# Where the input buffer and the weight tensors begin: a shift of 224 bytes in a two-block transformer kernel

## The chip, the cores and the metric

The kernel runs on one core of one Trainium2 chip. The metric is the device time of one execution in microseconds (us). A core has a matrix engine (TensorE, in the profile PE, and PEld for its loading of weights), VectorE (DVE), ScalarE (ACT), GpSimd (POOL) and a sync engine (SP) that issues most transfers. On-chip memory has 128 partitions; a tensor takes the same range of bytes in each, and its place in this text is the byte at which that range begins.

## The reference

Two transformer blocks on a sequence of 512 tokens of 1024 features, all in float32. Cut to what matters:

```python
def first_block(x, ...):
    h = rms_norm(x, norm_mix_pre)
    proj = h @ w_in                       # retention and sparse attention inputs
    mix = concatenate([retention(...), nsa(...)]) @ w_out
    x = x + rms_norm(mix, norm_mix_post)
    h = rms_norm(x, norm_ffn_pre)
    return x + rms_norm(conv_ffn(h, ffn_w_up, ffn_conv, ffn_w_down), norm_ffn_post)

def second_block(x, ...):
    for layer in range(2):                # 0: mLSTM and spatial gating, 1: latent attention
        x = x + mixer(rms_norm(x, ...))
        h = rms_norm(x, ...)
        x = x + square(relu(h @ ffn_w1)) @ ffn_w2
    return rms_norm(x, final_norm)
```

Most of the work is the dense products with the weight matrices.

## The kernel before

The features lie on the partitions and the 512 tokens along them, so an activation is eight tiles of 128 x 512. The weights are laid out beforehand as 296 panels of 128 x 1024 float32. They pass through a fixed line of four stations:

1. SyncE issues the transfer of a panel (512 KB, 4096 bytes for each partition) into slot `panel % 4` of `raw` (line 504), once VectorE is done with the panel that was there. The first four are issued by hand (lines 489 to 498), the first of them in two halves of 512 columns, between the eight tiles of the input `x_in`.
2. ScalarE copies the panel into a rounded high part, `w_hi` (`split`, line 1564), once TensorE has read the panel that held that half.
3. VectorE writes what the rounding lost, `w_lo = raw - w_hi` (`low`, line 2225).
4. TensorE multiplies. Each product of two float32 tiles is three matmuls, high x high, high x low and low x high (`product`, lines 695 to 697); a panel is eight such triples, 24 matmuls.

In nearly all products a 128 x 128 piece of the weights is the stationary operand, which is loaded ahead of the matmul, and an activation (`h_hi`, `h_lo`, `hid_hi`, `hid_lo`, ...) of 512 columns is the moving one. In those that yield values by tokens (`token_major`, line 723) it is the other way round. Tile names in the profile are "result<-operands"; of the two operands of a matmul the first is the moving one.

`w_hi` and `w_lo` have two halves each. Two more such buffers are free in parts of the kernel: `w_third` for the compression weights and for some panels ahead, `w_fourth` for panels ahead of the feed-forward and the gate. The compression matmuls (lines 1151 and 1152) take gathered activations `xg` as the stationary operand, of 126 and 62 columns, and `w_third` as the moving one.

Tensors are placed one behind another in the order in which `sb` makes them (lines 187 to 290). The places that matter here, modulo 256 bytes:

| tensor | begins past a multiple of 256 by, before | after |
|---|---|---|
| `small` | 128 | 128 |
| `masks`, `raw`, `w_hi`, `w_lo` | 224 | 0 |
| `ev`, `h_hi`, `h_lo`, `tmp`, `sq`, `x`, `hid_hi`, `hid_lo`, `q_hi`, `cq_hi` | 224 | 224 |
| `w_third`, `w_fourth` | 128 | 128 |
| `xg` | 0 | 0 |

Every piece of a weight tensor that a matmul reads begins a multiple of 512 bytes behind the tensor's start, so it has the same place modulo 256. `w_third` and `w_fourth` differ from `w_hi` because 8 spare columns (`front_spare`, `ahead_spare`) stand before them.

`small` holds the constants and gains by columns; its last 8, `g_mix_pre`, come in a transfer of their own before the rest, on ScalarE's queue (lines 1686 and 1687). The columns called `spare` in it are read by nothing. `masks` feeds small matmuls that add masks in the attention stages.

Of the kernel before, what the change touches and what calls it, by code (L numbers as in the profile page):

```python
# [13 lines left out]
F32 = mybir.dt.float32  # L14
# [7 lines left out]
P = 128  # L22
# [40 lines left out]
def columns(*parts):  # L63
    at, out = 0, {}
    for name, n in parts:
        out[name] = (at, n)
        at += n
    return out, at
# [3 lines left out]
    ("ident", 128), ("ones", 128), ("g_mix_post", 8), ("g_ffn_pre", 8), ("g_ffn_post", 8),  # L72
    ("gn", 4), ("cmp_pos", 64), ("conv0", 132), ("g_ab", 8), ("conv1", 40), ("gate_b", 1), ("g_head", 4),
    ("g_c", 8), ("g_cq", 3), ("g_ckv", 2), ("g_ffn1", 8), ("g_ffn2", 8), ("g_final", 8), ("freq", 1),
    ("rope_sign", 1), ("minus_half", 16), ("head_row", 4), ("shift_rows", 3), ("g_v", 4), ("spare", 57), ("g_mix_pre", 8))
FIRST, FIRST_N = columns(("rope_c", 512), ("rope_s", 512), ("cmp_c", 32), ("cmp_s", 32), ("decay", 2048))
SECOND, SECOND_N = columns(("sgu_b", 512), ("ws_t", 512))
MASKS, MASKS_N = columns(("ident", 128), ("k_q", 128), ("q_k", 128), ("cmp_q_k", 128), ("cmp_k_q", 512))
# [95 lines left out]
def build(nc, A):  # L174
    with ExitStack() as ctx:
        build_in(nc, A, ctx)


def build_in(nc, A, ctx):
    def sb(name, shape, dt, c=ctx):  # L180
        return c.enter_context(nc.sbuf_tensor(name, shape, dt))
# [7 lines left out]
    raw = sb("raw", [P, 4, PANEL], F32)  # L189
    w_hi = sb("w_hi", [P, 2, PANEL], F32R)  # L190
    w_lo = sb("w_lo", [P, 2, PANEL], F32R)
    ev = sb("ev", [P, 4, S], F32)
    h_hi = sb("h_hi", [P, KD, S], F32R)
    h_lo = sb("h_lo", [P, KD, S], F32R)
# [5 lines left out]
    spare = sb("spare", [P, 32], F32)  # L200
# [3396 lines left out]
```

## Time and profile before

| | |
|---|---|
| three runs, median (lowest to highest) | 1883.29 us (1883.24 to 1883.4) |
| the profiled execution: span from first to last instruction | 1881.6 us |
| what the median of the runs has over that span | 1.7 us |
| TensorE busy, share of the span | 98% |
| its loading of weights | 79% |
| VectorE, ScalarE, GpSimd | 61%, 40%, 12% |
| moved by the transfers | 165.68 MB, mean 88 GB/s |

The span is the profile's own time of one execution; the runs are timed from outside and include what lies around it. Busy TensorE doesn't mean TensorE at its peak, as matmuls are pipelined: how fast it works is read from the distance between the starts of neighbouring matmuls. The loading of weights (PEld) goes beside the matmuls.

### The profile page before, as it was taken

Reading aid. Unit: us, or ns where it says so; the run is one execution under the profiler, and the core shown is the slowest. Engines: PE = TensorE matmul, PEld = TensorE weight load, DVE = VectorE, ACT = ScalarE, POOL = GpSimd, SP = SyncE. Lnnn points to the kernel's source line nnn. Section 1 sums busy time; section 2 is a strip of 40 time slices with the busy share of each in tenths; the row PEclk is TensorE's granted clock in tenths of the full one; section 3 lists DMA queues with packets and bytes.
Section 4 is the critical chain, followed back from the end, with each engine's and each line's share of the span. In section 5 each row is a group of like instructions: output and inputs, shape, how many; then the busy total and the mean of one; then the engine's idle time right before and its main releaser. Section 6 shows DMA issues by size and latency. Waiting matters only on the chain.

```text
span 1881.6 us, 24672 instructions
## 1 busy us (share of the span) xinstructions
PE 1841.5 (98%) x8818; PEld 1481.6 (79%) x8818; DVE 1155.1 (61%) x1651; ACT 743.9 (40%) x1099; POOL 226.6 (12%) x228
## 2 busy tenths in 40 slices
PE   8999999999999999999999999999999999999998
PEld 6787558888888887887888888887666788888887
DVE  7867876784765778777543434476777553444344
ACT  6365334442432454655432232334544342323232
POOL 0021453000000030000000000003477200000000
PEclk9999999999999999999999999999999999999999
DMA  6332022233333233311333333332110123333332
GB/s 215 92 133 68 1 79 90 84 94 102 92 99 101 90 113 90 90 57 56 96 101 98 93 101 94 95 100 79 46 34 25 55 90 101 95 95 100 92 98 90
DMA packets 48217, 165.68 MB, mean 88 GB/s; under 512 B 5376, under 2 KB 7424, under 8 KB 48000
## 3 DMA queue, kind: packets, MB, share of 16 engines
q1 hardware_dynamic: 46512, 161.27, 28.3%
q10 hardware_dynamic: 1616, 3.22, 0.5%
q8 instruction: 56, 0.92, 0.2%
q14 instruction: 33, 0.27, 0.0%
HBM read 162.38 MB, written 2.10 MB: 87 GB/s over the span
## 4 chain that ended last, share of the span: by engine, by line
PE 85%; DVE 9%; ACT 3%; issue 2%; POOL 1%; DMA 0%; DVEq 0%; ACTq 0%; SPq 0%; POOLq 0%
PE ps L695 25%; PE ps L697 25%; PE ps L696 25%; PE ps L1089 2%; DVE w_lo L2225 1%; PE ps L989 1%; DVE qk_c L2995 1%; POOL x L608 1%; ACT w_hi L1564 1%; DVE tmp L2262 1%; PE ps L917 1%; PE ps L970 1%; PE ps L1059 1%; PE ps L1355 0%; PE ps L886 0%
## 5 line engine op out<-in xcount | busy, mean ns | idle before, releaser
L1564 ACT ACTIVATE w_hi<-raw 128x1024 fp32r<-128x1024 f32 x279 | 296.1, 1061 | 760.7 <-PE ps L697 760.4
L695 PE MATMUL ps<-h_hi,w_hi 128*128 128x512 f32 (+1 forms) x1288 | 507.9, 394 | 8.1 <-DVE w_lo L2506 7.6
L697 PE MATMUL ps<-h_hi,w_lo 128*128 128x512 f32 (+1 forms) x1288 | 499.0, 387 | 0.0
L696 PE MATMUL ps<-h_lo,w_hi 128*128 128x512 f32 (+1 forms) x1288 | 498.9, 387 | 0.0
L2225 DVE TENSOR_TENSOR w_lo<-raw,w_hi 128x1024 fp32r<-128x1024 f32 x279 | 345.5, 1238 | 119.7 <-ACT w_hi L1564 118.3
L695 PEld LDWEIGHTS ps<-h_hi,w_hi 128*128 128x128 f32 x1288 | 242.5, 188 | 62.1 <-DVE w_lo L2506 7.6
L697 PEld LDWEIGHTS ps<-h_hi,w_lo 128*128 128x128 f32 x1288 | 242.3, 188 | 50.0
L696 PEld LDWEIGHTS ps<-h_lo,w_hi 128*128 128x128 f32 x1288 | 242.6, 188 | 49.2 <-issue 1.9
L695 PE MATMUL ps<-hid_hi,w_hi 128*128 128x512 f32 (+1 forms) x716 | 273.6, 382 | 1.7 <-DVE w_lo L2225 0.9
L697 PE MATMUL ps<-hid_hi,w_lo 128*128 128x512 f32 (+1 forms) x716 | 272.6, 381 | 0.0
L696 PE MATMUL ps<-hid_lo,w_hi 128*128 128x512 f32 (+1 forms) x716 | 272.6, 381 | 0.0
L2440 DVE TENSOR_TENSOR x<-x,ps 128x512 f32<-128x512 f32 (+2 forms) x82 | 55.3, 675 | 187.9 <-PE ps L697 187.8
L695 PEld LDWEIGHTS ps<-hid_hi,w_hi 128*128 128x128 f32 x716 | 134.6, 188 | 29.0 <-DVE w_lo L2225 2.0
L696 PEld LDWEIGHTS ps<-hid_lo,w_hi 128*128 128x128 f32 x716 | 134.6, 188 | 25.8
L697 PEld LDWEIGHTS ps<-hid_hi,w_lo 128*128 128x128 f32 x716 | 134.6, 188 | 25.7
L3189 DVE SCALAR_TENSOR_TENSOR ev<-ps,tmp 128x512 f32<-128x512 f32 x64 | 44.1, 692 | 156.6 <-PE ps L697 152.9
L535 POOL TENSOR_TENSOR r<-r,small 128x2 f32<-128x2 f32 x6 | 4.2, 704 | 730.9 <-DVE r L2329 730.9
L530 POOL TENSOR_TENSOR r<-r,small 128x4 f32<-128x4 f32 x8 | 8.1, 1014 | 508.0 <-DVE r L2275 508.0
L2880 DVE TENSOR_REDUCE mla_negm<-ps 128x1 f32<-128x512 f32 x64 | 41.2, 686 | 15.6 <-PE ps L1059 14.9
L1875 ACT ACTIVATE pr<-ps 128x512 f32<-128x512 f32 x48 | 27.7, 597 | 52.9 <-PE ps L975 40.9
L2928 DVE TENSOR_TENSOR ev<-ps,tmp 128x512 f32<-128x512 f32 x44 | 30.4, 692 | 28.1 <-PE ps L697 26.6
L695 PE MATMUL ps<-w_hi,h_hi 128*128 128x512 f32 (+1 forms) x128 | 47.1, 368 | 0.3 <-DVE w_lo L2225 0.2
(435 smaller groups left out, 2547.6 us busy)
## 6 DMA issues: line engine op xcount, KB each, us to landing
raw<-in_panels SPq DMA_DIRECT2D x295, 512.0 KB, 3.6
x_in<-in_x SPq DMA_DIRECT2D x8, 256.0 KB, 5.5
x<-in_x ACTq DMA_DIRECT2D x1, 2048.0 KB, 9.7
out<-y SPq DMA_DIRECT2D x16, 128.0 KB, 1.8
first<-in_first SPq DMA_DIRECT2D x1, 1568.0 KB, 11.4
raw<-in_panels SPq DMA_DIRECT2D x2, 256.0 KB, 4.6
second<-in_second ACTq DMA_DIRECT2D x1, 512.0 KB, 3.5
small<-in_small ACTq DMA_DIRECT2D x1, 328.0 KB, 4.2
```

Of the source, the lines that this page charges most:

```text
L608: nc.gpsimd.tensor_tensor(x[:, k, at], x[:, k, at], tmp[:, k % 2, at], ALU.add).then_inc(x_ready, 1)
L695: nc.tensor.matmul(out, a[0], b[0], start=start, stop=False)
L696: nc.tensor.matmul(out, a[0], b[1], start=False, stop=False)
L697: return nc.tensor.matmul(out, a[1], b[0], start=False, stop=stop)
L1089: last = nc.tensor.matmul(ps[64 * a:64 * a + 64, pair_bank(p), cols_of(half)], mla_v[:, kt, n, :], weights_tile(n, kt)[:, cols_of(half)], ...
L1564: nc.scalar.activation(w_high(panel, i), raw[:, panel % 4, :], ACT.Copy).then_inc(w_hi_ready, 1)
L1875: nc.scalar.activation(prob(m), ps[:, 4 + m % 2, :], ACT.Exp, scale=0.125).then_inc(block_exp, 1)
L2225: signal(V.tensor_tensor(w_low(panel, i), raw[:, panel % 4, :], w_high(panel, i).bitcast(F32), ALU.subtract), w_lo_ready, wait=False)
L2440: signal(V.tensor_tensor(x[:, k, at], x[:, k, at], bank, ALU.add), done)
L2880: signal(V.tensor_reduce(mla_negm[:, n % 2, t:t + 1], ps[:, 2 + t % 2, :], AX.X, ALU.max, negate=True), mx_done, wait=False)
L2928: signal(V.tensor_tensor(src, bank, inv_b, ALU.mult), tile_out)
L3189: signal(V.scalar_tensor_tensor(ev[:, k % 4, :], bank, 0.0, inv_b, ALU.max, ALU.mult), tile_out, wait=False)
```

## The change

The unread columns `spare` in `small` shrink from 57 to 1, and a tensor of 56 float32 columns that nothing uses is put behind `w_lo`. So `masks`, `raw`, `w_hi` and `w_lo` begin 224 bytes earlier, and all tensors from `ev` on stay where they were. `g_mix_pre` moves with the end of `small`. No instruction is added, removed or put elsewhere; the transfer of `small` has 56 columns less.

```diff
@@ -72,7 +72,7 @@
     ("ident", 128), ("ones", 128), ("g_mix_post", 8), ("g_ffn_pre", 8), ("g_ffn_post", 8),
     ("gn", 4), ("cmp_pos", 64), ("conv0", 132), ("g_ab", 8), ("conv1", 40), ("gate_b", 1), ("g_head", 4),
     ("g_c", 8), ("g_cq", 3), ("g_ckv", 2), ("g_ffn1", 8), ("g_ffn2", 8), ("g_final", 8), ("freq", 1),
-    ("rope_sign", 1), ("minus_half", 16), ("head_row", 4), ("shift_rows", 3), ("g_v", 4), ("spare", 57), ("g_mix_pre", 8))
+    ("rope_sign", 1), ("minus_half", 16), ("head_row", 4), ("shift_rows", 3), ("g_v", 4), ("spare", 1), ("g_mix_pre", 8))
@@ -189,6 +189,7 @@
     raw = sb("raw", [P, 4, PANEL], F32)
     w_hi = sb("w_hi", [P, 2, PANEL], F32R)
     w_lo = sb("w_lo", [P, 2, PANEL], F32R)
+    behind_weights = sb("behind_weights", [P, 56], F32)
     ev = sb("ev", [P, 4, S], F32)
     h_hi = sb("h_hi", [P, KD, S], F32R)
```

## Rows read from the trace of the kernel before

**Rows 1.** The page: its first lines, and the chain that ended last.
```profile
span 1881.6 us, 24672 instructions
PE 1841.5 (98%) x8818; PEld 1481.6 (79%) x8818; DVE 1155.1 (61%) x1651; ACT 743.9 (40%) x1099; POOL 226.6 (12%) x228
...
PE 85%; DVE 9%; ACT 3%; issue 2%; POOL 1%; DMA 0%; DVEq 0%; ACTq 0%; SPq 0%; POOLq 0%
PE ps L695 25%; PE ps L697 25%; PE ps L696 25%; PE ps L1089 2%; DVE w_lo L2225 1%; PE ps L989 1%; DVE qk_c L2995 1%; POOL x L608 1%; ACT w_hi L1564 1%; DVE tmp L2262 1%; PE ps L917 1%; PE ps L970 1%; PE ps L1059 1%; PE ps L1355 0%; PE ps L886 0%
```

**Rows 2.** Waits: waiter <- releaser, us in total, times, longest us; SPq is SyncE's queue.
```profile
ACT w_hi L1564 <- PE ps L697: 760.4, 234, 7.5
ACT h_hi L1613 <- DMA raw<-in_panels: 2.2, 1, 2.2
SPq L504 <- DVE w_lo L2225: 1591.5, 277, 94.7
```

**Rows 3.** Timeline, TensorE, 512 columns: start us, duration us, instruction; first, last of seven.
```profile
1699.94 0.39 PE L695 MATMUL ps<-h_hi,w_hi 128*128 128x512 f32 x1
...
1701.30 0.39 PE L695 MATMUL ps<-h_hi,w_hi 128*128 128x512 f32 x1
```

**Rows 4.** The same, 256 columns, weights in w_hi and w_lo; first and last of ten.
```profile
301.02 0.28 PE L696 MATMUL ps<-h_lo,w_hi 128*128 128x256 f32 x1
...
302.10 0.28 PE L696 MATMUL ps<-h_lo,w_hi 128*128 128x256 f32 x1
```

**Rows 5.** Instructions with w_hi: x count, duration ns min/median/max, first and last start.
```profile
L695 PEld LDWEIGHTS ps<-h_hi,w_hi x1288: 186/188/334, 7.6 to 1825.5; 128*128 128x128 f32 x184
...
L695 PE MATMUL ps<-hid_hi,w_hi x716: 278/389/499, 409.7 to 1871.1; 128*128 128x512 f32 x165, 128*128 128x256 f32 x14
...
L695 PE MATMUL ps<-w_hi,h_hi x128: 290/389/470, 33.7 to 788.5; 128*128 128x512 f32 x96, 128*128 128x288 f32 x32
...
L695 PE MATMUL ps<-aq_hi,w_hi x64: 389/389/501, 871.7 to 918.7; 128*128 128x512 f32 x64
```

**Rows 6.** Timeline, 256 columns, weights in w_third and w_fourth; first and last of 31.
```profile
694.79 0.28 PE L695 MATMUL ps<-h_hi,w_third 128*128 128x256 f32 x1
...
698.39 0.28 PE L695 MATMUL ps<-h_hi,w_third 128*128 128x256 f32 x1
```

**Rows 7.** Timeline, xg stationary, w_third moving: first of eight, and the matmul behind them.
```profile
135.70 0.28 PE L1151 MATMUL ps<-w_third,xg 128*126 128x256 f32 x1
...
136.63 0.39 PE L695 MATMUL ps<-h_hi,w_hi 128*128 128x512 f32 x1
```

**Rows 8.** Timeline, 512 columns, just after a stall; first and last of six.
```profile
704.24 0.40 PE L695 MATMUL ps<-h_hi,w_hi 128*128 128x512 f32 x1
...
705.40 0.39 PE L697 MATMUL ps<-h_hi,w_lo 128*128 128x512 f32 x1
```

**Rows 9.** Instructions that read raw: duration ns min/median/max.
```profile
L1564 ACT ACTIVATE w_hi<-raw x279: 1042/1063/1072, 9.5 to 1859.3; 128x1024 fp32r<-128x1024 f32 x140
L2225 DVE TENSOR_TENSOR w_lo<-raw,w_hi x279: 1210/1226/2183, 10.6 to 1860.5; 128x1024 fp32r<-128x1024 f32 x140
L1564 ACT ACTIVATE w_third<-raw x11: 1042/1064/1070, 63.9 to 677.4; 128x1024 fp32r<-128x1024 f32 x11
L2225 DVE TENSOR_TENSOR w_third<-raw,w_third x11: 1209/1224/1227, 65.4 to 678.5; 128x1024 fp32r<-128x1024 f32 x11
```

**Rows 10.** Transfers by line: x count, KB each, median us from issue to landing.
```profile
raw<-in_panels SPq DMA_DIRECT2D x295, 512.0 KB, 3.6
...
small<-in_small ACTq DMA_DIRECT2D x1, 328.0 KB, 4.2
```

**Rows 11.** The chain of the start: start us, us, what.
```profile
1.20 4.07 DMA raw<-in_panels
...
7.62 0.80 PE ps L695
```

**Rows 12.** Stretch: us, busy (x) of PE, PEld, DVE, ACT, POOL, clock, DMA share, GB/s.
```profile
0.00:8.00 8.00, 0.38 (x1) 0.38 (x2) 1.79 (x3) 3.81 (x6) 1.54 (x8) 1.00 0.79 269
```

## The prediction

> **What bounds the kernel now.** I read the profile from the outside in: shares of engines, waits by engine, then the single matmuls, because a change that moves operands and nothing else can only act through the duration of single instructions and transfers. TensorE is busy 98% of a span of 1881.6 us, and 85% of the chain that ended last is on it [rows 1]. Three quarters of that chain is one helper, lines 695 to 697. The engines that prepare the weights wait for it: ScalarE's copy into `w_hi` waits 760.4 us for TensorE's readings, 234 times, so some 3.2 us before each; the transfers of panels wait 1591.5 us for VectorE to free a slot of `raw`. For a transfer instructions wait only at the start, the longest 2.2 us, once [rows 2]. So the reader is to see a queue in which weights are always early, and one thing that counts: how long TensorE takes per matmul.
>
> In a quiet stretch six matmuls of 512 columns take 1701.30 - 1699.94 = 1.36 us, 226.7 ns each [rows 3]. With 256 columns nine take 302.10 - 301.02 = 1.08 us, 120.0 ns each [rows 4]. The difference, 106.7 ns for 256 columns, is one column per cycle at 2.4 GHz; 226.7 less twice that leaves 13.3 ns, and so does 120.0 less once that: a surcharge per matmul, whatever its length. This surcharge is what the change could touch: if it were the price of where an operand begins, it would be worth tens of microseconds.
>
> **The change, part by part.** `spare` inside `small` goes from 57 to 1 columns, 56 x 4 = 224 bytes, and `behind_weights` puts 224 bytes back behind `w_lo`. `masks`, `raw`, `w_hi` and `w_lo` move down by 224 bytes; before they began 224 bytes past a multiple of 256, now on one. `ev`, `h_hi`, `hid_hi` and the rest stay 224 past. No instruction, wait or queue changes.
>
> (a) **Weights as the stationary operand**, 1288 + 716 + 64 = 2068 triples, 6204 matmuls [rows 5] (and some smaller groups). The trace has tensors at another place already: `w_third` and `w_fourth` lie 128 past a multiple of 256. With them as weights and `h_hi`, `h_lo` moving, thirty matmuls of 256 columns take 698.39 - 694.79 = 3.60 us, 120.0 ns each [rows 6], the same as with `w_hi` [rows 4]. Moving the weights by 96 bytes against the moving operand cost and brought nothing. A place at 256 itself is shown by `xg` alone (it begins on a multiple of 256), stationary under `w_third`: eight matmuls of 256 columns take 136.63 - 135.70 = 0.93 us, 116 ns [rows 7]. Those load 126 and 62 columns, not 128, so I don't read the 4 ns as alignment; they are the lower bound: 4 x 6204 = 25 us at most. The upper bound is a cadence as after a stall, 5 matmuls in 705.40 - 704.24 = 1.16 us, 232 ns [rows 8]: 5.3 x 6204 = +33 us. I take 0, by rows 6, nearest in size, operands and engine. The load itself lasts 188 ns [rows 5] beside a matmul of 226.7 ns, so 39 ns of cover are left; a load shorter by any amount brings nothing.
>
> (b) **Weights as the moving operand**: 128 triples, 384 matmuls [rows 5] (and a few of the third block). Here the moving operand itself lands on 256. Bound: all 13.3 ns go, 384 x 13.3 = 5.1 us; or, as in (a), +5.3 ns, 2.0 us. I take 0: `w_third` is the moving operand of rows 7, and 9.3 ns of surcharge are still there.
>
> (c) **ScalarE and VectorE.** ScalarE's copy has a median of 1063 ns into `w_hi`, 1064 into `w_third`; VectorE's difference 1226 and 1224 [rows 9]. Both read `raw` and write elsewhere, and a shift of the one side by 96 bytes moves them by 2 ns or less. Cover: the 3.2 us before each copy. If it were gone, both hold about 1% of the chain each [rows 1]; even 2% of some 38 us is 0.8 us. I take 0.
>
> (d) **Transfers.** A panel lands 3.6 us after its issue [rows 10], with four slots and a panel of 24 x 226.7 ns = 5.4 us of matmuls; steady transfers are hidden, and a faster one starts the next no sooner, as the queue waits for VectorE. On the path is the first half panel alone, 4.07 us from issue to landing [rows 11], with everything after it up to the first matmul at 7.62 us. It shares the engines with the transfer of `small`, now 300 KB instead of 328 [rows 10]: 28 KB at the 269 GB/s of that stretch [rows 12] are 0.1 us. Bounds: nothing, if that transfer is not in its way, and 0.4 us, a tenth of the landing. I take -0.1.
>
> The trace cannot show how a transfer treats a destination off 256, as nothing large is written on one. The Trainium skill, "DMA: Bandwidth & Descriptors", section "How a descriptor splits into AXI transactions", says that a transfer off a 256-byte boundary pays for the bytes before its start. By it a row of 2048 bytes would go from 71 beats to 64 and the start would gain up to 0.4 us, an estimate from that page; the sum would be 1882.9 instead of 1883.2.
>
> (e) `masks` feed small matmuls of 128 columns and less in the attention stages, `small` keeps its start. 0.
>
> **Sum.** 1881.6 - 0.1 = 1881.5 us of span. The median of three runs, 1883.29, lies 1.7 us above the span; I keep that: 1883.2 us. What a measurement of this kernel can tell from no change is 0.2%, 3.8 us.
>
> **The rivals.**
> - *The surcharge is the stationary operand's place.* 13.3 ns x 6204 = 83 us would go, 1883.3 - 83 = 1800; with the 4 ns of rows 7, 1858. For: a surcharge that doesn't grow with the length looks like a start cost. Against: rows 4 and 6, equal at two places, and 39 ns of cover over the load. Chance 0.03. The Trainium skill, "TensorE: Matmul & The Clock Gate", section "Wait — 56ns, not 53.3ns?", has a surcharge of only 2.5 ns, which leaves room for such a cost; by it the gain would be 10.8 x 6204, about 67 us, an estimate from that page.
> - *The moving operand's place counts.* Only (b) gains: 1883.2 - 5.1 = 1878.1. For: a matmul reads its moving operand at its own pace, with no cover. Against: rows 7. Chance 0.07.
> - *Slower: two reading streams out of step.* Before, stationary and moving operand lie equal modulo 256; after, 224 bytes apart. If the loads beside the matmuls then meet the moving reads at a bad distance and break the cadence, each of 6204 matmuls takes up to 5.3 ns more [rows 8]: 1916. It decides from 0.6 ns on (3.8 us / 6204). For: 224 apart is in no row. Against: rows 6, where they are 96 apart at 120.0 ns. Chance 0.07.
> - *Nothing moves*, as allocation rounds the two edits differently: 1883.3, no difference. Chance 0.02.
> - *The forecast*: chance 0.81; own range 1882.4 (the 0.8 us of (c) and the start) to 1884.5.
>
> **How the numbers follow.** Within 0.2%: 0.81 + 0.02, less 0.03 for small unseen effects that pass the bound, 0.80. Faster 0.03 + 0.07, and 0.02 of those: 0.12. Slower 0.07 + 0.01: 0.08. The range reaches from the forecast's own toward the small ends of the rivals: down to 1880.0, a good half of (b)'s 5.1 us, up to 1885.0, a quarter of a nanosecond per matmul slower (0.25 x 6204 = 1.6 us). Outside are the large effects, 2 in 10 with what the rivals hold.
>
> **What would show it.** In the profile after, the same quiet stretch should have 226.7 ns per matmul and 120.0 at 256 columns (right for a), `w_hi` as moving operand the same as before (b), medians of 1063 and 1226 ns within 3 ns (c), the first half panel landed in 3.7 to 4.07 us and the first matmul at 7.2 to 7.6 us (d). A matmul spacing other than 226.7 by over 0.6 ns, either way, makes the forecast wrong, and nothing else in the kernel can.

## The result, and the profile after

The changed kernel takes 1919.95 us (median of 4 runs, 1919.79 to 1920.1), the kernel before 1883.35 us: a ratio of 1.0192, 95% interval 1.0179 to 1.0204. It is slower by 36.6 us. The forecast of no change was wrong; the time is within 4 us of what the rival "two reading streams out of step" gave (1916).

The first lines of the page after, and its chain:

```profile
span 1918.2 us, 24672 instructions
PE 1879.9 (98%) x8818; PEld 1483.5 (77%) x8818; DVE 1155.1 (60%) x1651; ACT 742.2 (39%) x1099; POOL 226.4 (12%) x228
...
PE 91%; DVE 5%; ACT 2%; issue 2%; POOL 0%; DMA 0%; DVEq 0%; ACTq 0%; SPq 0%; POOLq 0%
```

Beside [rows 1] the counts of instructions are the same, and VectorE, ScalarE and GpSimd are as busy as before within 2 us. TensorE alone is busy for 38.4 us more. The same instructions take longer on one engine.

Which ones, the timeline says. TensorE in a quiet stretch after, 512 columns (start us, duration us, instruction; six matmuls from the first to the last line):

```profile
1735.87 0.40 PE L696 MATMUL ps<-h_hi,w_hi 128*128 128x512 f32 x1
...
1737.27 0.40 PE L696 MATMUL ps<-h_hi,w_hi 128*128 128x512 f32 x1
```

1.40 us by 6 are 233.3 ns, against 226.7 in [rows 3]: the surcharge over the 213.3 ns of 512 columns goes from 13.3 to 20 ns. With 256 columns it shrinks instead, 20 matmuls from 304.52 to 306.88 us, 118.0 ns each, against 120.0 in [rows 4]:

```profile
304.52 0.28 PE L697 MATMUL ps<-h_lo,w_hi 128*128 128x256 f32 x1
...
306.88 0.28 PE L696 MATMUL ps<-h_hi,w_hi 128*128 128x256 f32 x1
```

The view by stretches counts it over a quarter of a millisecond. The kernel before, TensorE, two stretches (us, busy (x count), granted clock, DMA share, GB/s):

```profile
1000.00:1250.00 250.00, 250.00 (x1105) 1.00 0.32 97
1550.00:1800.00 250.00, 250.00 (x1105) 1.00 0.33 97
```

The changed kernel has 1073 in both; the second of them:

```profile
1550.00:1800.00 250.00, 249.56 (x1073) 1.00 0.32 94
```

TensorE is idle for 0.44 us at most, at the same granted clock (1.00 of 2.4 GHz), and gets through 32 matmuls fewer. Two of each count reach over the edges: 250 us by 1103 are 226.7 ns, by 1071 are 233.4. From here on this count is the ruler; "1105" is the pace of the kernel before, "1073" that of the changed one. The two agree with the total: 6204 matmuls by 6.6 ns are 41 us, or 39 us without the 264 of them that have 256 columns; and the starts of all matmuls of 512 columns that read `w_hi` or `w_lo` lie 227.1 ns apart on average before and 233.3 after (distances over 250 ns, which are waits, left out; 6320 distances before), 39 us too. Those in the attention stages had no steady pace before either, and the last 2 us are not traced.

The work beside the matmuls is not the cause. In the changed kernel 1790 matmuls of 512 columns with stationary weights run while ScalarE, VectorE and GpSimd are all idle, and 377 of those also while no transfer moves: they take 233.3 and 233.4 ns on average, against 226.7 and 226.8 before. So the cost needs no other engine and no transfer. Nor does it reach products of two activations, whose places didn't change: the matmuls of `q_lo` with `k_hi` and of `q_hi` with `k_lo` take 231.7 and 231.3 ns before, 231.0 and 230.8 after.

Nothing changed in the rest, as the prediction had it. Instructions that read `raw`, after (duration ns min/median/max):

```profile
L1565 ACT ACTIVATE w_hi<-raw x279: 1040/1061/1069, 9.7 to 1895.8; 128x1024 fp32r<-128x1024 f32 x140
L2226 DVE TENSOR_TENSOR w_lo<-raw,w_hi x279: 1211/1226/2185, 10.8 to 1896.9; 128x1024 fp32r<-128x1024 f32 x140
```

These are the medians of [rows 9] within 2 ns. The chain of the start, after:

```profile
1.20 4.03 DMA raw<-in_panels
...
7.58 0.80 PE ps L696
```

The first half panel lands 0.04 us earlier than in [rows 11], and TensorE starts 0.04 us earlier. Right behind the start TensorE is still slow, and there its pace is the same as before the change, where six matmuls take 2.56 us too (from 8.64 to 11.20 us). The timeline after:

```profile
8.60 0.63 PE L698 MATMUL ps<-h_hi,w_lo 128*128 128x512 f32 x1
...
11.16 0.63 PE L698 MATMUL ps<-h_hi,w_lo 128*128 128x512 f32 x1
```

Six matmuls in 2.56 us are 427 ns each, 512 columns at the lower of the two clock levels, 1.2 GHz, with no surcharge at all (the clock column of the view by stretches prints 1.00 here; the level is read from the pace). At that level the change costs nothing.

### The profile page after: what moved, and what is told of

Its sections match the earlier page's. It is cut to its first block, busy times and chain, and to the rows that moved or that the text cites. A ratio compares the mean times of both kernels' runs of the same rounds, so it can differ in the third digit from the quotient of the medians.

```text
span 1918.2 us, 24672 instructions
## 1 busy us (share of the span) xinstructions
PE 1879.9 (98%) x8818; PEld 1483.5 (77%) x8818; DVE 1155.1 (60%) x1651; ACT 742.2 (39%) x1099; POOL 226.4 (12%) x228
## 4 chain that ended last, share of the span: by engine, by line
PE 91%; DVE 5%; ACT 2%; issue 2%; POOL 0%; DMA 0%; DVEq 0%; ACTq 0%; SPq 0%; POOLq 0%
PE ps L696 28%; PE ps L697 27%; PE ps L698 27%; PE ps L1090 2%; PE ps L990 1%; PE ps L1356 1%; PE ps L918 1%; PE ps L971 1%; PE ps L1060 1%; PE ps L887 0%; PE ps L1103 0%; ACT w_hi L1565 0%; PE ps L959 0%; DVE w_lo L2226 0%; PE ps L976 0%
## 5 line engine op out<-in xcount | busy, mean ns | idle before, releaser
L696 PE MATMUL ps<-h_hi,w_hi 128*128 128x512 f32 (+1 forms) x1288 | 514.6, 400 | 7.8 <-DVE w_lo L2507 7.6
L698 PE MATMUL ps<-h_hi,w_lo 128*128 128x512 f32 (+1 forms) x1288 | 506.4, 393 | 0.0
L697 PE MATMUL ps<-h_lo,w_hi 128*128 128x512 f32 (+1 forms) x1288 | 506.4, 393 | 0.0
L696 PE MATMUL ps<-hid_hi,w_hi 128*128 128x512 f32 (+1 forms) x716 | 277.6, 388 | 1.5 <-DVE w_lo L2226 0.9
L698 PE MATMUL ps<-hid_hi,w_lo 128*128 128x512 f32 (+1 forms) x716 | 276.8, 387 | 0.0
L697 PE MATMUL ps<-hid_lo,w_hi 128*128 128x512 f32 (+1 forms) x716 | 276.8, 387 | 0.0
```

The costliest lines, as they stand in the source:

```text
L696: nc.tensor.matmul(out, a[0], b[0], start=start, stop=False)
L697: nc.tensor.matmul(out, a[0], b[1], start=False, stop=False)
L698: return nc.tensor.matmul(out, a[1], b[0], start=False, stop=stop)
```

## The experiments

Theory 1: the distance between the stationary and the moving operand, modulo 256 bytes, sets the pace. Theory 2: weights that begin on a multiple of 256 are slow by themselves. Theory 3: what fills or reads `raw` at its new place disturbs the matmuls. All ratios are to runs of the kernel before on the same chip (medians 1883.35 to 1884.59 us), with 95% intervals. In the table, distance is the place of the stationary weights less that of the moving activations, modulo 256, from -128 to 127; matmuls is the count of TensorE in the stretch 1550 to 1800 us.

| kernel | weights, moving, modulo 256 | distance | median us | ratio (interval) | matmuls |
|---|---|---|---|---|---|
| before | 224, 224 | 0 | 1883.35 | 1 | 1105 |
| after | 0, 224 | +32 | 1919.95 | 1.0192 (1.0179 to 1.0204) | 1073 |
| all_down | 0, 0 | 0 | 1883.38 | 0.9999 (0.9988 to 1.001) | 1105 |
| rest_up | 224, 0 | -32 | 1919.69 | 1.0192 (1.0162 to 1.0221) | 1074 |
| w192 | 192, 224 | -32 | 1919.8 | 1.0192 (1.0163 to 1.0222) | 1073 |
| w128 | 128, 224 | -96 | 1920.96 | 1.0198 (1.0169 to 1.0228) | 1073 |
| w160 | 160, 224 | -64 | 1896.63 | 1.0063 (1.0034 to 1.0092) | 1094 |
| w96 | 96, 224 | -128 | 1915.87 | 1.0169 (1.0125 to 1.0212) | 1079 |
| w32 | 32, 224 | +64 | 1919.85 | 1.0187 (1.0157 to 1.0216) | 1073 |
| w208 | 208, 224 | -16 | 1890.78 | 1.0033 (1.0017 to 1.0048) | 1097 |
| plus16 | 16, 0 | +16 | 1916.6 | 1.0172 (1.0143 to 1.0202) | 1075 |
| minus4 | 220, 224 | -4 | 1904.41 | 1.0108 (1.0078 to 1.0137) | 1073 |
| h_up256 | 224, 224 (h 256 higher) | 0 | 1883.6 | 1.0 (0.9988 to 1.0012) | 1105 |

**Distance or place.** all_down leaves out the filler behind the weights, so that everything moves:

```diff
-    ... ("spare", 57), ("g_mix_pre", 8))
+    ... ("spare", 1), ("g_mix_pre", 8))
```

> Everything behind the constants begins 224 bytes earlier, so weights and moving operands both begin on a multiple of 256 and their distance is 0 as in the kernel before. Theory 1 (the distance between the stationary and the moving operand modulo 256 sets the pace): 226.7 ns per matmul of 512 columns, about 1883 us. Theory 2 (a weight tensor that begins on a multiple of 256 is slow by itself): 233.3 ns, about 1920 us.

rest_up keeps `spare` at 57 and puts 8 columns behind the weights:

```diff
     w_lo = sb("w_lo", [P, 2, PANEL], F32R)
+    behind_w_lo = sb("behind_w_lo", [P, 8], F32)
```

> Weights and input buffer stay 224 past a multiple of 256, all tensors behind them move up by 32 bytes and begin on one. Theory 1: the distance is no longer 0, so 233 ns and about 1920 us, or something between if the size of the distance (32 bytes) matters. Theory 2: the weights are where they were, 1883 us.

The stretch 1550 to 1800 us of all_down:

```profile
1550.00:1800.00 250.00, 250.00 (x1105) 1.00 0.32 97
```

The same stretch of rest_up:

```profile
1550.00:1800.00 250.00, 249.57 (x1074) 1.00 0.32 94
```

All tensors on multiples of 256 are as fast as all of them 224 past one; weights left where they were are slow as soon as their partners move. Theory 2 falls by both, theory 1 stands.

**How far.** The split of 57 filler columns between `spare` and the tensor behind the weights moves masks, input buffer and weights alone: `spare` 49 in w192, 41 in w160, 33 in w128, 25 in w96, 9 in w32, the rest behind `w_lo`. For w192:

```diff
-    ... ("spare", 57), ("g_mix_pre", 8))
+    ... ("spare", 49), ("g_mix_pre", 8))
...
     w_lo = sb("w_lo", [P, 2, PANEL], F32R)
+    behind_w_lo = sb("behind_w_lo", [P, 8], F32)
```

> Weights, masks and input buffer 32 bytes earlier than before, at 192 past a multiple of 256; the rest stays. Theory 1: the same distance as with the rest moved up by 32, so the same time as that kernel (about 1920 us or between). Theory 2: 1883 us, as 192 is no multiple of 256.

> The same at 128 past a multiple of 256, the place of the third and fourth weight buffers, 96 bytes from the moving operands. Theory 1: about 1920 us, with an uneven spacing at 256 columns like that of the third and fourth buffers. Theory 2: 1883 us.

> Weights at 160 past a multiple of 256, distance 64 bytes to the moving operands. If the modulus of theory 1 is 64: 226.7 ns and 1883 us. If it is 128 or more, or any distance but 0 counts: 233 ns and 1920 us.

> Weights at 96 past a multiple of 256, distance 128 bytes. If the modulus is 64 or 128: 1883 us. If it is 256 or more: 1920 us.

> Weights at 32 past a multiple of 256, so 64 bytes above the moving operands modulo 256 (192 below them). Measured so far: 64 below gives 1897, 128 gives 1916, 96 below and 32 to either side 1920 to 1921. If the pace depends on the size of the distance modulo 256: about 1897. If the sign counts too, or the modulus is larger than 256: another time, up to 1920.

w192 has the time of rest_up, which shares its distance of -32 and none of its places: theory 1 again. But the size of the distance doesn't order the times. -64 costs a third of what -32 and -96 do, between the two times that its expectation allowed, and +64 costs all of it: at 64 the sign counts, while at 32 both signs cost the same. The sign shows inside one trace too, because where `w_hi` and `w_lo` are the moving operands the distance has the opposite sign: in w160 those matmuls, at +64, take 233.2 ns on average, those with stationary weights, at -64, 229.1. The stretch of w160, between the two paces:

```profile
1550.00:1800.00 250.00, 250.00 (x1094) 1.00 0.33 96
```

**Which tensor.** raw_only puts the 56 columns behind `raw`, raw_high behind `w_hi`, with `spare` at 1 in both:

```diff
     raw = sb("raw", [P, 4, PANEL], F32)
+    behind_raw = sb("behind_raw", [P, 56], F32)          # raw_only
     w_hi = sb("w_hi", [P, 2, PANEL], F32R)
+    behind_w_hi = sb("behind_w_hi", [P, 56], F32)        # raw_high
```

> The 56 columns stand behind raw: masks and raw begin on a multiple of 256, the weight tensors stay at 224. Theory 1: TensorE doesn't read raw, so 226.7 ns and 1883 us, within 0.2%. Theory 3 (the writers and transfers at the new place of raw disturb the matmuls): toward 1920 us.

> The 56 columns stand behind w_hi: masks, raw and w_hi begin on a multiple of 256, w_lo stays at 224. If it is the load of the next stationary piece that meets the reads of the running matmul, two loads in three are displaced (high, high, low): matmuls of line 696 and of line 698 (counted as in this file) at 233 ns, those of line 697, beside which the low part is loaded, at 227; 1883 + 2/3 of 37 = 1908 us. If each matmul meets its own stationary piece instead, the short one is line 698. If one displaced tensor spoils the cadence as a whole: 1920 us.

raw_only takes 1885.05 us, a ratio of 1.0002 (0.999 to 1.0013), with 1105 matmuls in the stretch: theory 3 falls, and the new places of `masks` and `raw` cost nothing. raw_high takes 1911.9 us, 1.0148 (1.0104 to 1.0191), between the 1908 of "two loads in three" and 1920. Its stretch, 232 ns:

```profile
1550.00:1800.00 250.00, 250.00 (x1078) 1.00 0.32 94
```

No single line is spared. By the distances between starts over the whole trace a matmul with `hid` takes 232.1 ns on line 696, 230.6 on line 697 and 233.3 on line 698. The shortest is the one beside which `w_lo`, the tensor in step, is loaded, as expected of "the load of the next piece". But it is far from 227, and the order proves little: in w128, where both tensors are displaced alike, the same three lines take 236.8, 230.8 and 232.5 ns, and line 697 is the shortest there too. What raw_high shows is that one displaced tensor spoils most of the cadence of the others.

**The load beside the matmul.** narrow_0 and narrow_224 leave out part of the computation: in the dense products the correction of 64 of 128 outputs by the low part of the moving operand. The load for it takes 64 columns and lasts 134 ns instead of 188.

```diff
-            nc.tensor.matmul(out, a[0], b[1], start=False, stop=False)
+            nc.tensor.matmul(out[0:64], a[0][:, 0:64], b[1], start=False, stop=False)
```

> Placement of the kernel before. In the dense products the second of the three matmuls takes 64 columns of the stationary piece and writes 64 partitions; the correction of the other 64 by the low part of the moving operand is left out. So the load beside the first matmul of each triple is half as long. No cost of the distance here: first matmul 226.7 ns, as in the kernel before, and 1883 us if a narrow matmul keeps the pace by itself.

> The same edit and omission with the changed placement. Theory 1a (the reads of the next load collide with the moving reads of the running matmul for as long as the load lasts): the first matmul of each triple loses half its extra 6.6 ns, 230 ns, the others stay at 233; the kernel about 12 us (2068 x 3.3 ns = 7, to twice that) faster than the changed one. Theory 1b (a cost per matmul that is there whatever the load beside it): 233 ns for all, 1920 us.

narrow_224 takes 1912.05 us, 7.9 us less than the changed kernel and inside what theory 1a gave. In a triple with `hid` the first matmul, beside which the short load runs, is 229.5 ns ahead of the next on average, not 233.5; the second takes 231.1 and the third 235.0, on average 233. The matmul beside the shorter load is the shortest one. Its timeline (nine matmuls in 2.09 us, 232 ns):

```profile
1712.40 0.39 PE L702 MATMUL ps<-hid_hi,w_hi 128*128 128x512 f32 x1
1712.63 0.39 PE L703 MATMUL ps<-hid_lo,w_hi 128*64 128x512 f32 x1
...
1714.49 0.39 PE L702 MATMUL ps<-hid_hi,w_hi 128*128 128x512 f32 x1
```

narrow_0 was to show nothing and showed the most. With no distance, less work for the loads makes the kernel slower: 1898.64 us, 1.0074 (1.0045 to 1.0104). Its stretch:

```profile
1550.00:1800.00 250.00, 250.00 (x1089) 1.00 0.32 96
```

That is 230 ns. So a shorter load doesn't by itself mean a shorter matmul: 226.7 ns looks like a rhythm which loads of equal length keep and a load of another length breaks. It also weakens narrow_224 as evidence: the edit changes the rhythm by itself, and the three matmuls of a triple differ by 6.0 ns in w128 without any narrow load. The first matmul's 4.0 ns fit a cost that lies beside the load and don't show it.

**Small distances and the modulus.** w208 and minus4 have both weight tensors in one, at an offset of 4 and 7 columns, and `spare` at 49; plus16 the same at 4 columns, with 64 columns of room and `spare` at 1. For w208:

```diff
-    w_hi = sb("w_hi", [P, 2, PANEL], F32R)
-    w_lo = sb("w_lo", [P, 2, PANEL], F32R)
+    w_both = sb("w_both", [P, 4 * PANEL + 8], F32R)
+    w_hi = w_both[:, 4:4 + 2 * PANEL].rearrange("p (a b) -> p a b", a=2)
+    w_lo = w_both[:, 4 + 2 * PANEL:4 + 4 * PANEL].rearrange("p (a b) -> p a b", a=2)
```

> Weights 16 bytes below the moving operands, closer than any distance tried, and no multiple of 32. If only distance 0 is in step: 1920. If what counts is the start in a line of 32 bytes or more: 1883. If the 13 ns surcharge that is left at distance 0 is itself a collision that a small distance avoids: below 1883.

> Weights 16 bytes above the moving operands modulo 256 (at 16 and 0). Theory 1 with the size of the distance alone: as 16 below, 228 ns and 1889 us. If the sign counts, as it did between 64 below (1897) and 64 above (1920): slower than 16 below, up to 1920.

> Weights 4 bytes, one element, below the moving operands. If each byte of distance adds from 0 on: about 226.7 + a quarter of 1.3 ns, 1885 us. If any distance but 0 breaks the step: 1889 us or more. If lines of 16 bytes or wider count: 1883 us, or 1889 if a start off a multiple of 16 counts by itself.

h_up256 puts three small tensors, 256 bytes together, ahead of `ev` instead of behind `sq` (`ones_r`, which lay between them, moves by 160 bytes):

```diff
     w_lo = sb("w_lo", [P, 2, PANEL], F32R)
+    r4 = sb("r4", [P, 6, 4], F32)
+    root_parts = sb("root_parts", [P, 2, 4], F32R)
+    spare = sb("spare", [P, 32], F32)
```

> Places modulo 256 as in the kernel before, but ev, h_hi, h_lo, tmp and sq begin 256 bytes higher; hid_hi and hid_lo stay. If the modulus is 256: 226.7 ns everywhere, 1883 us. If it is 512 or more: products with h at about 233 ns, those with hid at 226.7, about 1883 + 1288 x 3 x 6.6 ns = 1908 us.

h_up256 shows the modulus: a distance of 256 is none, and w96 showed that 128 is one. plus16 against w208 shows the sign again, 1916.6 against 1890.78 us. None of them is below 1883, and closer is not better: -4 costs three times what -16 does. The oddest is minus4. Its two stretches:

```profile
1000.00:1250.00 250.00, 250.00 (x1105) 1.00 0.33 97
1550.00:1800.00 250.00, 250.00 (x1073) 1.00 0.32 95
```

Both are the same kind of work, a feed-forward of the second block with the same tensors, and both paces hold unbroken in one execution: 226.7 ns in the first, 233.3 in the second. w208 has two paces as well, 226.7 and 228.3 ns:

```profile
450.00:650.00 200.00, 200.00 (x884) 1.00 0.33 96
1000.00:1250.00 250.00, 250.00 (x1097) 1.00 0.32 95
```

Its change from 228.3 to 226.7 falls into one unbroken stream of matmuls with `hid`, at 422 us, right behind a single distance of 305 ns; another of 281 ns, at 399 us, changed nothing. So one placement allows several rhythms, and a short pause can tip it from one to another; what decides between them is open.

## Why the prediction was wrong

- **What bounds the kernel** was right: TensorE's time per matmul is all that counts, and the price of a nanosecond on it (6204 matmuls) carries the whole difference.
- **(a), stationary weights at 0**, is the step that failed. It put the cost at 0 where 6.6 ns for each matmul of 512 columns were measured, 36.6 us of the kernel. It took the value of rows 6, "nearest in size, operands and engine", where `w_third` at a distance of -96 runs at 120.0 ns as `w_hi` does in rows 4. The rows were read rightly and don't carry over. w128 puts the main weights at the same distance of -96 and has 1073 matmuls in the stretch, 233.4 ns each, but with 256 columns it keeps its pace as well (18 matmuls in 2.16 us, 120.0 ns each):

```profile
304.61 0.28 PE L696 MATMUL ps<-h_hi,w_hi 128*128 128x256 f32 x1
...
306.77 0.28 PE L696 MATMUL ps<-h_hi,w_hi 128*128 128x256 f32 x1
```

So at one placement the column count decides whether the distance costs anything, and rows 6 had 256 columns where nearly all of the 6204 matmuls have 512. Why it does is argued only: with 256 columns a load (188 ns in rows 5) lasts longer than the distance between matmuls (120 ns), so loads are in flight all the time, with 512 columns (226.7 ns) they pause. The rows held a hint too: the starts within rows 6 are uneven by 0.01 to 0.02 us, which I averaged away.
- "The load itself lasts 188 ns beside a matmul of 226.7 ns, so 39 ns of cover are left" was wrong as an argument. In the changed kernel a load lasts 187 to 188 ns as before and ends 45 ns ahead of the next one, and yet each matmul takes 233.3 ns: a load that is over in time is no sign that it costs nothing.
- **The bound above, rows 8**, was no bound: 5.3 ns, taken from the cadence after a stall, and 6.6 measured; 33 us, and 36.6 measured. That the rival's sum, 1916, comes so near to 1919.95 is in part luck, as nothing shows that the two cadences have one cause. The rival's mechanism, two operands out of step modulo 256, is what the runs bear out. It had a chance of 0.07 because only rows 6 spoke on it.
- **(b)**: `w_hi` as the moving operand lost like the rest (233.5 ns on average, 226.7 before), it didn't gain.
- **(c), (d), (e)** held: medians within 2 ns, the first landing 0.04 us earlier where 0.1 was taken, nothing from `masks` (raw_only). The 0.04 us tell nothing, though: that landing takes between 3.65 us (rest_up) and 4.13 us (plus16) in the traces of this case. And `masks` also feeds 24 matmuls of 512 columns, not only the small ones that (e) names.
- By the Trainium skill, "DMA: Bandwidth & Descriptors", section "How a descriptor splits into AXI transactions", as the prediction reads it, the start would have gained up to 0.4 us, an estimate from that page. At the start no run shows such a gain. In the steady transfers the direction agrees: the median landing of a panel is 3.54 to 3.56 us in the six traces with `raw` on a multiple of 256 and 3.58 in the four with `raw` 224 past one.
- The Trainium skill, "SBUF — State Buffer", section "Who interferes with whom", gives TensorE two independent read ports, one for the moving operand and one for loading weights, and says that it never waits on anyone. The measurement differs: the place of one operand relative to the other is worth 1.9% here, with all other engines idle too (233.3 ns against 226.7). Whether the two meet in the memory, in a port or behind it, no run shows.

What stays open: the mechanism. Shown are that the paces which occur depend on the distance modulo 256, that its sign counts at 16 and 64, and that the pace has several steady values. No placement tried has a steady pace below 226.7 ns, so what the remaining 13.3 ns of surcharge are stays open too. That these are reads of two streams which meet in the same part of the memory at a bad moment is argued from that, not shown; narrow_224 and raw_high fit it but don't decide it. Why -64 costs a third and +64 all, and why -4 costs more than -16, is not explained.

## What to carry to other kernels

Where matmuls of 512 float32 columns stream back to back and each loads new weights, keep the stationary and the moving operands at the same place modulo 256 bytes; where they lie together didn't matter at the two places tried, 224 and 0. A tensor of odd size put in front of the one and not of the other cost up to 2% here, with no instruction changed, so compare the distance between starts of matmuls in a quiet stretch after every change of the layout. A row of the trace of another column count is no evidence for this one: w128 keeps 120.0 ns at 256 columns and loses 6.6 ns per matmul at 512.

## What the runs showed of the hardware

- The pace of back-to-back matmuls of 512 float32 columns, each with a load of its own, takes steady values between 226.7 and 233.3 ns, depending on the two operands' places; right behind the start, at the lower clock level, it is 427 ns at either place.
- Near is not harmless, and the sign counts: -16 costs 0.3% (1.0033, 1.0017 to 1.0048), -4 costs 1.1% (1.0108), +16 costs 1.7% (1.0172).
- With 256 columns the change makes the matmuls no slower: 118.0 ns in place of 120.0.
- A shorter load can slow a well-placed kernel: narrow_0, loads of 134 ns among those of 188, 230 ns per matmul in place of 226.7.
- One placement can run at two paces in one execution: minus4 at 226.7 and 233.3 ns, w208 at 226.7 and 228.3.
